# The beginning of a hybrid block kernel, rebuilt: statistics tile by tile, normalisation and splitting on two engines, small loads moved

## The reference, cut to what matters

```
h = layer_norm(concat(pad, meta, x), ln_in_g, ln_in_b)
proj = h @ w_in[l]                       # XM, OG, i, f, QA, KA, VA, GA, GB
y_m = mlstm_branch(xm, o_pre, i_pre, f_pre, ...)
y_a = diff_attn_branch(qa, ka, va, ...)
merged = sigmoid(ga) * (y_m @ w_branch_m) + sigmoid(gb) * (y_a @ w_branch_a)
h = layer_norm(DN_ALPHA * h + merged @ w_out, ln1_g, ln1_b)
ffn = group_moe(h, w_router, router_bias, w_gate_e, w_up_e, w_down_e)   # 16 experts
h = layer_norm(DN_ALPHA * h + ffn, ln2_g, ln2_b)
```

## Time and profile before

| what | value |
|---|---|
| median of 3 runs | 835.6 us (834.52 to 838.2) |
| the profiled execution, its time | 835.89 us |
| its span | 834.1 us |
| PE busy | 779.0 us, 93% |
| DVE, ACT, POOL busy | 357.6, 240.8, 22.7 us |
| read from HBM | 249.91 MB, 301 GB/s over the span |

### The profile page before, as it was taken

One profiled execution on the slowest core, in us unless ns is written; L12 is line 12 of the kernel. 1 busy time (PEld: TensorE's weight loads), 2 busy tenths in 40 slices (PEclk: granted clock), 3 DMA queues, 4 the chain that ended last, 5 costly groups with the idle time before them and its releaser, 6 DMA issues.

```text
span 834.1 us, 12681 instructions
## 1 busy us (share of the span) xinstructions
PE 779.0 (93%) x4496; PEld 474.1 (57%) x4497; DVE 357.6 (43%) x780; ACT 240.8 (29%) x523; POOL 22.7 (3%) x51
## 2 busy tenths in 40 slices
PE   4999999999999999998999999889999998898993
PEld 3998679999889999783333333333333333333331
DVE  6677436554665787636223212230223202312225
ACT  2454433444766655431111011101111111011010
POOL 2002000000001000000000000000000000000000
PEclk9999999999999999979999999999999999999997
DMA  8965050553105433995999999999999999999971
GB/s 252 388 233 200 2 202 2 201 199 139 68 1 202 152 130 151 393 384 240 429 427 428 427 427 428 428 428 429 429 428 427 428 429 429 428 427 427 427 329 50
DMA packets 36764, 251.30 MB, mean 301 GB/s; under 512 B 5921, under 2 KB 13170, under 8 KB 23426
## 3 DMA queue, kind: packets, MB, share of 16 engines
q1 hardware_dynamic: 34416, 250.76, 73.0%
q10 hardware_dynamic: 2322, 0.21, 0.2%
HBM read 249.91 MB, written 1.05 MB: 301 GB/s over the span
## 4 chain that ended last, share of the span: by engine, by line
PE 71%; DMA 21%; DVE 3%; ACT 2%; issue 2%; POOL 1%; DVEq 0%; POOLq 0%; SPq 0%; ACTq 0%
PE ps L1952 26%; DMA raw<-in_w_down_e_dram 21%; PE ps L1617 8%; PE ps L1619 7%; PE ps L1618 7%; PE ps L1905 2%; PE ps L1913 2%; PE ps L1673 1%; PE ps L1920 1%; PE ps L1669 1%; PE ps L1729 1%; PE ps L1592 1%; PE ps L1868 1%; PE ps L1870 1%; PE ps L1869 1%
## 5 line engine op out<-in xcount | busy, mean ns | idle before, releaser
L1952 PE MATMUL ps<-raw,hid 128*64 128x512 f32 x512 | 119.6, 618 | 19.4 <-DMA raw<-in_w_down_e_dram 18.9
L1617 PE MATMUL ps<-hi_h,whi 128*128 128x256 f32 (+1 forms) x448 | 129.8, 290 | 3.8 <-DVE wlo L983 3.7
L1619 PE MATMUL ps<-hi_h,wlo 128*128 128x256 f32 (+1 forms) x448 | 127.5, 285 | 0.0
L1618 PE MATMUL ps<-lo_h,whi 128*128 128x256 f32 (+1 forms) x448 | 127.2, 284 | 0.0
L1952 PE MATMUL ps<-raw,xg 128*64 128x512 f32 x512 | 112.7, 592 | 1.7 <-DVE xg L1413 1.7
L983 DVE TENSOR_TENSOR wlo<-raw,whi 128x512 fp32r<-128x512 f32 x144 | 93.4, 690 | 46.7 <-ACT whi L688 44.1
L1544 DVE TENSOR_TENSOR gs<-ps,gsig 128x512 f32<-128x512 f32 x16 | 11.1, 692 | 183.0 <-ACT gsig L930 182.2
L1617 PEld LDWEIGHTS ps<-hi_h,whi 128*128 128x128 f32 x448 | 84.4, 188 | 8.3 <-DVE wlo L983 4.8
L1952 PEld LDWEIGHTS ps<-raw,hid 128*64 128x64 f32 x512 | 36.7, 141 | 92.0 <-issue 65.3
L688 ACT CAST whi<-raw 128x512 fp32r<-128x512 f32 (+1 forms) x144 | 83.2, 618 | 13.2 <-PE ps L1619 11.9
L1619 PEld LDWEIGHTS ps<-hi_h,wlo 128*128 128x128 f32 x448 | 84.5, 189 | 0.0
(11 more groups left out here) (321 smaller groups left out, 1017.9 us busy)
## 6 DMA issues: line engine op xcount, KB each, us to landing
raw<-in_w_down_e_dram SPq DMA_DIRECT2D x32, 2048.0 KB, 21.2
raw<-in_w_gate_e_dram SPq DMA_DIRECT2D x16, 2048.0 KB, 25.7
raw<-in_w_up_e_dram SPq DMA_DIRECT2D x16, 2048.0 KB, 23.8
gate_x<-in_w_gate_e_dram SPq DMA_DIRECT2D x16, 2048.0 KB, 27.2
raw<-in_w_in_dram SPq DMA_DIRECT2D x28, 1024.0 KB, 9.2
up_x_right<-in_w_up_e_dram SPq DMA_DIRECT2D x16, 1024.0 KB, 27.6
up_x_left<-in_w_up_e_dram SPq DMA_DIRECT2D x8, 2048.0 KB, 25.2
raw<-in_w_branch_m_dram SPq DMA_DIRECT2D x4, 1024.0 KB, 8.1
```

The source lines that it names most:

```text
L1617: mm(o, w1, hi[:, k, c0:c0 + n], start=(k == 0), stop=False)
L1618: mm(o, w1, lo[:, k, c0:c0 + n], start=False, stop=False)
L1619: last = mm(o, w2, hi[:, k, c0:c0 + n], start=False, stop=(k == KB - 1))
L1952: last = mm(ps[r0:r0 + SLOTS, bank_no, :], lhs[:, k % 4, k // 4, :], w[:, k % 2, 512 * c:512 * c + 512], start=(k == 0), stop=(k == KB - 1))
```

## The change

On DVE the statistics of the meta tile and the first token tile go ahead, and POOL raises these two (in one instruction over 128 rows) while DVE takes the third tile's. The first token tile is normalised by ACT, with the bias `nmr0`, the other two by DVE. ACT's mask casts come first. The first weight block is split ahead of the tokens on both engines. `hfull` has four buffers; DVE makes the even ones and ACT the odd ones. On PE `keep_warm` stands ahead of the transposes, which write other banks, and the first block waits for `lo_h` one k at a time. The split of `wif`, the sums for `lams` and the waits for them stand behind XM's stream. The nine small loads go from ACT's queue to SP's, between XM's quarters and `rows_in`; the residual (`hres`) comes one block later. Its core as a diff:

```diff
     rows_in = at("rows_in", [P, 2, D], F + 12288)
-    hfull = at("hfull", [P, 2, S], F + 20480)
+    HB = 4
+    hfull = at("hfull", [P, HB, S], F + 55616)
+    nmr0 = at("nmr0", [P, 1], F + 59968)
...
-                sp.wait_ge(raw_in[0][0], 16)
+                with nc.allow_non_contiguous_dma(reason="a few short vectors"):
+                    sp.dma_start(wif[:], w_in[0, :, 2048:2056].rearrange("(k p) c -> p k c", p=P)).then_inc(s.wif_in, 16)
+                    sp.dma_start(gate_bias[:, 0:1], b_i.rearrange("a h -> h a")).then_inc(s.gb_in, 16)
+                    sp.dma_start(gate_bias[:, 1:2], b_f.rearrange("a h -> h a")).then_inc(s.gb_in, 16)
+                    for tile, v in ((gain4, ln1_g), (bias4, ln1_b)):
+                        sp.dma_start(tile[:], v[0].rearrange("(c i a) -> i c a", c=2, a=4)).then_inc(s.gain4_in, 16)
+                for j, v in enumerate((lam_q1, lam_q2, lam_k1, lam_k2)):
+                    sp.dma_start(lamv[:, j, :], v[0].partition_broadcast(P)).then_inc(s.lam_in, 16)
                 for j, v in enumerate((ln_in_g, ln_in_b)):
                     sp.dma_start(rows_in[:, j, :], v.partition_broadcast(P)).then_inc(s.rows_in_in, 16)
...
+        pool.wait_ge(s.var_ready, 2)
+        pool.tensor_tensor(rstd[:, 0:2], ve[:, 0:2], minus_half[:, 0:2], ALU.pow).then_inc(s.rstd_ready, 1)
         pool.wait_ge(s.var_ready, 3)
-        pool.tensor_tensor(rstd[0:META, 0:1], ve[0:META, 0:1], minus_half[0:META, 0:1],
-                           ALU.pow).then_inc(s.rstd_ready, 1)
-        pool.tensor_tensor(rstd[:, 1:3], ve[:, 1:3], minus_half[:, 1:3], ALU.pow).then_inc(s.rstd_ready, 1)
+        pool.tensor_tensor(rstd[:, 2:3], ve[:, 2:3], minus_half[:, 2:3], ALU.pow).then_inc(s.rstd_ready, 1)
 
...
-        with nc.allow_non_contiguous_dma(reason="a few short vectors"):
-            for tile, v in ((gain4, ln1_g), (bias4, ln1_b)):
-                act.dma_start(tile[:], v[0].rearrange("(c i a) -> i c a", c=2, a=4)).then_inc(s.gain4_in, 16)
-            act.dma_start(wif[:], w_in[0, :, 2048:2056].rearrange("(k p) c -> p k c", p=P)).then_inc(s.wif_in, 16)
-            act.dma_start(gate_bias[:, 0:1], b_i.rearrange("a h -> h a")).then_inc(s.gb_in, 16)
-            act.dma_start(gate_bias[:, 1:2], b_f.rearrange("a h -> h a")).then_inc(s.gb_in, 16)
-        for j, v in enumerate((lam_q1, lam_q2, lam_k1, lam_k2)):
-            act.dma_start(lamv[:, j, :], v[0].partition_broadcast(P)).then_inc(s.lam_in, 16)
-
-        for k in range(KB):
-            act.wait_ge(s.h_full, k + 1)
-            act.copy(hi_h[:, k, :], hfull[:, k % 2, :]).then_inc(s.h_hi, 1)
+        act.wait_ge(s.consts, 1)
+        for narrow, wide in ((ident_b, ident), (late_b, late), (ahead_b, ahead), (before_b, before)):
+            act.copy(narrow[:], wide[:]).then_inc(s.masks_ready, 1)
+        act.wait_ge(s.nmr0_ready, 1)
+        act.activation(xt[:, 1, :], xt[:, 1, :], ACT.Identity, bias=nmr0[:], scale=rstd[:, 1:2]).then_inc(s.x1_ready, 1)
+
...
+        def full_half(k):
+
+            act.wait_ge(s.ht_t, k + 1)
+            if k >= HB:
+                act.wait_ge(s.h_lo, k - HB + 1)
+            act.activation(hfull[:, k % HB, :], ps[:, 4 + k % 4, 0:S], ACT.Identity, bias=chan[:, C_LNB + k:C_LNB + k + 1],
+                           scale=chan[:, C_LNG + k:C_LNG + k + 1]).then_inc(s.h_odd, 1)
+
+        def high_half(k):
+            act.wait_ge(s.h_odd if k % 2 else s.h_even, k // 2 + 1)
+            act.copy(hi_h[:, k, :], hfull[:, k % HB, :]).then_inc(s.h_hi, 1)
+
+        act.wait_ge(s.chan_ready, 1)
+        for k in range(0, KB, 2):
+            full_half(k + 1)
+            high_half(k)
+            high_half(k + 1)
+
+        stream(XM, OG)
+
         act.wait_ge(s.wif_in, 16)
-        act.wait_ge(s.consts, 1)
-        for narrow, wide in ((ident_b, ident), (late_b, late), (ahead_b, ahead),
-                             (before_b, before)):
-            act.copy(narrow[:], wide[:]).then_inc(s.masks_ready, 1)
         act.copy(wif_hi[:, :, 0:MH], wif[:, :, MH:2 * MH]).then_inc(s.wif_split, 1)
         act.copy(wif_hi[:, :, 32:32 + MH], wif[:, :, 0:MH]).then_inc(s.wif_split, 1)
-
-
-        stream(XM, OG)
-
         act.wait_ge(s.lam_sum, 1)
         act.activation(lams[:, 2:4], lams[:, 0:2], ACT.Exp).then_inc(s.lam_exp, 1)
...
+        rows = (META, P, P)
+
+        def tile_stats(j):
+            n = rows[j]
             dve.wait_ge((s.x_in0, s.x_in1, s.x_in2)[j], 16)
             for c in range(2):
                 own(dve.bn_stats(stats[0:n, j, c, :], xt[0:n, j, 512 * c:512 * c + 512]))
...
+
+        def tile_mean(j):
+            own(dve.bn_aggr(mv[0:rows[j], j, :], stats[0:rows[j], j, :, :]))
+
+        def tile_var(j):
+            dve.tensor_scalar(ve[0:rows[j], j:j + 1], mv[0:rows[j], j, 1:2], EPS, None, ALU.add).then_inc(s.var_ready, 1)
+
+        def tile_norm(j):
+            n = rows[j]
             dve.tensor_scalar(xt[0:n, j, :], xt[0:n, j, :], mv[0:n, j, 0:1], rstd[0:n, j:j + 1],
                               ALU.subtract, ALU.mult).then_inc(s.xn_ready, 1)
+
+        tile_stats(0)
+        tile_stats(1)
+        own.settle()
+        tile_mean(0)
+        tile_mean(1)
+        own.settle()
+        dve.wait_ge(s.consts, 1)
+        tile_var(0)
+        tile_var(1)
+        tile_stats(2)
+        dve.wait_ge(s.rstd_ready, 1)
+        dve.scalar_tensor_tensor(out=nmr0[:], in0=mv[:, 1, 0:1], scalar=-1.0, in1=rstd[:, 1:2], op0=ALU.mult,
+                                 op1=ALU.mult).then_inc(s.nmr0_ready, 1)
+        own.settle()
+        tile_mean(2)
+        own.settle()
+        tile_var(2)
+        tile_norm(0)
         dve.wait_ge(s.rows_t, 1)
-        dve.tensor_copy(chan[:], ps[:, 7, 0:81]).then_inc(s.chan_ready, 1)
+        dve.tensor_copy(chan[:], ps[:, 3, 0:81]).then_inc(s.chan_ready, 1)
+        dve.wait_ge(s.rstd_ready, 2)
+        tile_norm(2)
         dve.wait_ge(s.chan_ready, 1)
         own(dve.tensor_scalar(chan[:, C_AG:C_AG + 1], chan[:, C_AG:C_AG + 1], 1.0 - LAM_INIT, None, ALU.mult))
 
 
+        def full_half(k):
+
+            dve.wait_ge(s.ht_t, k + 1)
+            dve.tensor_scalar(hfull[:, k % HB, :], ps[:, 4 + k % 4, 0:S], chan[:, C_LNG + k:C_LNG + k + 1],
+                              chan[:, C_LNB + k:C_LNB + k + 1], ALU.mult, ALU.add).then_inc(s.h_even, 1)
+
         def low_half(k):
             dve.wait_ge(s.h_hi, k + 1)
-            dve.tensor_tensor(lo_h[:, k, :], hfull[:, k % 2, :], hi_h[:, k, :].bitcast(F32),
+            dve.tensor_tensor(lo_h[:, k, :], hfull[:, k % HB, :], hi_h[:, k, :].bitcast(F32),
                               ALU.subtract).then_inc(s.h_lo, 1)
 
...
         def split(section, blk, odd):
 
             for kh in range(2):
...
         split(XM, 0, 0)
-        dve.wait_ge(s.wif_split, 2)
-        for a, b in ((0, MH), (32, 0)):
-            own(dve.tensor_tensor(wif_lo[:, :, a:a + MH], wif[:, :, b:b + MH],
-                                  wif_hi[:, :, a:a + MH].bitcast(F32), ALU.subtract))
-        own.settle()
-        dve.sem_inc(s.wif_split, 1)
-
-        dve.wait_ge(s.lam_in, 64)
-        own(dve.tensor_tensor(lamp[:], lamv[:, 0:2, :], lamv[:, 2:4, :], ALU.mult))
-        own.settle()
-        dve.tensor_reduce(lams[:, 0:2], lamp[:], AX.X, ALU.add).then_inc(s.lam_sum, 1)
-
+        full_half(0)
+        full_half(2)
+        for k in range(0, KB, 2):
+            low_half(k)
+            low_half(k + 1)
+            if k + HB < KB:
+                dve.wait_ge(s.h_lo, k + 1)
+                full_half(k + HB)
...
+            n = blk - 3
...
-                dve.wait_ge(s.xn_ready, t + 2)
+                dve.wait_ge(s.xn_ready, 2)
+                dve.wait_ge(s.x1_ready, 1)
                 dve.tensor_tensor(hres[:, t, :], xt[:, t + 1, :], rows_in[:, 0, :], ALU.mult).then_inc(s.hres_scaled, 1)
 
         stream(XM, OG, residual)
 
+        dve.wait_ge(s.wif_split, 2)
+        for a, b in ((0, MH), (32, 0)):
+            own(dve.tensor_tensor(wif_lo[:, :, a:a + MH], wif[:, :, b:b + MH],
+                                  wif_hi[:, :, a:a + MH].bitcast(F32), ALU.subtract))
+        own.settle()
+        dve.sem_inc(s.wif_split, 1)
+
+        dve.wait_ge(s.lam_in, 64)
+        own(dve.tensor_tensor(lamp[:], lamv[:, 0:2, :], lamv[:, 2:4, :], ALU.mult))
+        own.settle()
+        dve.tensor_reduce(lams[:, 0:2], lamp[:], AX.X, ALU.add).then_inc(s.lam_sum, 1)
+
+        dve.wait_ge(s.masks_ready, 4)
...
-        pe.wait_ge(s.xn_ready, 3)
+        pe.transpose(ps[:, 3, 0:81], crow[:], ident[0:81, 0:81]).then_inc(s.rows_t, 1)
+        keep_warm(2, 16)
+        pe.wait_ge(s.xn_ready, 2)
+        pe.wait_ge(s.x1_ready, 1)
         for k in range(KB):
             if k >= 4:
-                pe.wait_ge(s.h_full, k - 3)
+                pe.wait_ge(s.h_odd if k % 2 else s.h_even, (k - 4) // 2 + 1)
             c = slice(P * k, P * k + P)
-            pe.transpose(ps[:, k % 4, 0:META], xt[0:META, 0, c], ident[0:META, 0:META])
```

(24 more changed lines are left out.)

54 lines of the change are left out of this document (21 added, 33 removed).

## The result

The changed kernel takes 830.88 us (median of 6 runs, 829.26 to 832.18), the kernel before 835.12 us on the same chip (6 runs, 832.76 to 838.2). The medians are 4.2 us apart, 0.5%. The ratio of the runs is 0.9942, with an interval of 0.9918 to 0.9967, so the change is faster, by some 0.6%. The profiled execution took 831.87 us with a span of 830.1, which is 4.0 less than before. The time forecast was 832.4, in a range of 829.6 to 835.2.

What follows compares the result with a forecast made beforehand. PE, busy for 93% of the span, was taken as the bound. From the profiled 835.9 us, -6.3 (XM earlier) +1.4 (OG) +1.7 (clock) = -3.2 gave 832.7, or 832.4 against the median, in a range of 829.6 to 835.2.

Steps and rivals of the forecast that it cites:

- T: Start of the first transpose on PE, forecast at 13.2 us, right behind `keep_warm`, 1.2 us later than before.
- The statistics: DVE, POOL and ACT ahead of the transposes: tiles ready at 10.8, 1.2 us earlier, worth nothing because `keep_warm` hides them.
- The give-back at OG: Between XM and OG: `wif` and `lams` work, formerly free, now costs 1.4 us, bounds nothing and 1.5.
- ACT's wait for `lam_sum`: Sign to look for behind XM's last evacuation: ACT waits about 1.1 us for `lam_sum`.
- absolute date behind OG: Stages behind OG: none found whose start doesn't depend on PE, so the shift should reach the end.
- T + 7.5: End of XM's first block, 0.4 us behind the last `lo_h`; 20.9 instead of 27.2, so XM ends 6.3 us earlier.
- 0.2 more for the second block's weights: XM's second block: its weights are split only behind the first block's `lo_h`, put at 0.2 us.
- I expect it to fall behind them, and XM's first block to run partly at 1.2 GHz: 1.7 us: PE's clock falls behind the transposes, slowing XM's first block; cost 1.7 us, bounds nothing and 3.4.
- the fall at 361: Earlier clock fall at about 361 us, behind transposes and short products during which PE counts as busy.
- the first rival: The clock holds from the transposes into XM, no 1.7 us loss: 831.0, or 830.7 at the median; chance 0.30.
- the third: Shift swallowed by a later stage's own start or dearer clock falls; time stays 834 to 836.5, chance 0.13.
- The small loads: SP's queue ahead of OG's quarters: counted as nothing, 3.4 us of room before OG's fourth quarter is needed at 40.2.

Runs made afterwards that it cites:

- old_stats: Changed kernel with statistics and normalisation as before the change, all three tiles normalised by DVE; one run, 830.83 us.
- aside: Changed kernel with the `wif` and `lams` work put among XM's blocks instead of behind XM; 828.67 us, ratio 0.9926 to the kernel before.
- transposes3: Changed kernel with each group of transposes issued three times into the same bank; one run, 836.37 us.
- no_warm: Changed kernel without the 16 products of `ident` (`keep_warm`) ahead of the transposes; 832.09 us, ratio 0.9959 to the kernel before.
- warm8: Changed kernel with 8 instead of 16 products of `ident` in `keep_warm`; 830.0 us, ratio 0.9937 to the kernel before.
- dve_full: Changed kernel with all eight `hfull` made by DVE again, ACT only casting, four buffers kept; one run, 830.43 us.
- after_again: The changed kernel itself with no edit, measured again on another chip; 831.38 us, ratio 0.9951 to the kernel before.
- small_on_act: Changed kernel with the nine small loads back on ACT's queue, at the beginning; one run, 831.09 us.
- warm_behind: Changed kernel with `keep_warm` back behind the transposes, all else as changed; 835.89 us, ratio 0.9986 to the kernel before.
- aside_warm10_fill: `aside_warm10` plus 3 and 5 products of `ident` in PE's two waits at the router; 828.65 us, ratio 0.9911 to the kernel before.
- aside_warm10: `aside` with 10 instead of 16 products of `ident` in `keep_warm`; 829.61 us, ratio 0.9928 to the kernel before.
- whole_lo: Changed kernel, but PE waits for all eight `lo_h` before XM's first product; one run, 838.23 us.

## Why the forecast came out as it did

**Held.** `keep_warm` holds the transposes: T 13.24, forecast 13.2. The statistics are hidden under it: the tiles were ready at 9.98 (forecast 10.8), and `old_stats` shows that they are worth nothing there. The give-back at OG is 1.46 (forecast 1.4, bounds 0 and 1.5), and `aside` shows that it is paid in full. ACT's wait for `lam_sum` is 1.12 (forecast 1.1). There is no absolute date behind OG that swallows the shift: 5.41 us at OG's end are 5.5 at the turning of `h1`.

**Mis-sized.** The step "T + 7.5" for the first block, with 0.2 more for the second block's weights. XM ended 6.86 us earlier, not 6.3. The forecast let the splitting set the first block's end, with the last `lo_h` at T + 7.1. It was done at T + 6.25 (19.49), since two `lo_h` take 0.78 us together and not 1.01, and a pair of k 1.17 and not 1.5. What sets the end is PE: eight groups of transposes at 0.53 take 4.1 us, 24 products at 0.126 take 3.0, together 7.1, and the evacuation follows at T + 7.36. PE is the bound itself, because the clock was up for the transposes. Laid out from the two timelines, XM's first product comes 6.89 us earlier by 5.65 of `keep_warm` no longer behind the transposes, and 2.47 by the transposes at full clock, less 1.23 for the later T. The 2.47 is a term that the forecast did not have; it had the first block's 3.0 hidden under the splitting in its place. When DVE makes all `hfull`, the splitting does set it, at T + 8.19.

**Failed.** The step "I expect it to fall behind them, and XM's first block to run partly at 1.2 GHz: 1.7 us". The clock held through the transposes and all of XM. The row it was drawn from was read too widely: 6.5 us of transposes had not raised a low clock, and I took this to say that they let a high one fall. `transposes3` separates the two. The other row, the fall at 361, was behind transposes too, but behind short products between waits as well; it doesn't say which of them counted. One of its readings was off as well, without effect: the products of `ident` were at the low clock until 23.0 (4.4 us behind 18.54), not until about 22.

**Why the total was near all the same.** A clock loss of the same 1.7 us came at another place, the first expert's products (8.79 against 7.09). From the profiles: -6.86 at XM, +1.46 at OG, +1.7 at 374, which makes -3.7; measured -4.0, the rest in small steps between. The forecast had -6.3, +1.4, +1.7. So the number is near in part by luck: the first rival (the clock holds, 831.0) described the beginning, and the third (falls at dearer places) described the router, at its smallest price. Against the medians the forecast was further off: 830.88 was measured, the forecast said 832.4, and the first rival 830.7, with a chance of 0.30. The time below 831.4 had a chance of 0.38.

That loss goes with the low stretches; that it belongs to the change as such is not shown, and `aside`, with the same beginning, has the length of the kernel before. From the turning of `h1` to the second expert's gather it takes 31.29 us before (386.18 less 354.89) and 32.91 after. Over the profiles of all kernels this length falls into steps, and it follows the time that the granted clock is low between 350 and 385 us:

| length, us | clock low, us | kernels |
|---|---|---|
| 29.7 | 6.8 | `no_warm`, `transposes3` |
| 31.2 to 31.3 | 10.2 | before, `warm8`, `aside`, `dve_full` |
| 32.7 to 33.0 | 13.7 | changed, `after_again`, `old_stats`, `small_on_act`, `warm_behind`, `aside_warm10_fill` |
| 34.6 | 17.1 | `aside_warm10`, `whole_lo` |

None of these edits, apart from `aside_warm10_fill`'s, touches that part of the program. From the first length to the last it is 4.95 us in three steps, 1.65 each for 3.4 us more at the low clock, the price of one short low stretch. So the low clock accounts for the lengths; what sets its time is open. They mask gains of that size: `warm8` ends OG 1.8 us earlier than the changed kernel and has a median 0.9 lower (on another chip).

**The small loads.** Right in the result, close in the room. OG's quarters are issued 2.6 us later (20.26 against 17.66). `wif` and the first `gate_bias` hold SP for 2.83 and 3.46 us, until 16.1, but that is not what the move cost: in the kernel before SP was held as well, until 16.8, by the plain `rows_in`, the first load behind XM's quarters there:

```profile
11.77 5.02 SPq L460 DMA_DIRECT2D rows_in<-in_ln_in_g_dram  x1
```

Nearly all of the delay is the issue time of the other seven, 3.2 us (16.12 to 19.31), less the 0.7 by which SP was free earlier. In the changed kernel's DMA view the fourth is

```profile
raw<-in_w_in_dram SPq DMA_DIRECT2D x1, 1024.0 KB, 14.9
```

issued at 23.9: it lands at 38.8, not at 36.8, and is needed at about 39.6. Of the 3.4 us of room 0.8 are left. In `warm8` they are used up: ACT's cast of OG's first block stands idle for 1.21 us, until 39.08, as the quarter lands. OG's end is 1.83 us earlier all the same (66.89), as is XM's, so even there it set nothing.

**What stays open.** Why the low stretches at the router come where they do was not shown: the filled waits and the vanished second stretch are one profile each with and without, and later stretches changed along with it. The beginnings, too, are single profiles of each kernel, and no run has the old statistics behind a shorter `keep_warm`. Nor was `whole_lo`'s wait filled, which would tell whether the clock falls there without idleness.

## What to carry to other kernels

Look at what stands in the bounding engine's own queue before pricing anything on others: here a filler of 6.4 us hid all gains in statistics and normalisation, and in one profile half of it did the same job. Look for edits that need each other: with the filler back behind the transposes XM ends 4.4 us later, and with PE waiting for all operands at once, in place of one k at a time, it takes 5 us longer from T. Either one taken away leaves 2.3 to 2.5 of the 6.9 us at XM's end, so the two can't be added. Work that was free behind a filler isn't free in its new place: put it among the blocks of a stream, not at its end, where it cost 1.5 us in full.

## What was unexpected in the hardware

- **Transposes held a clock that they had not raised.** 12.5 us of them at full pace with the clock up (`transposes3`), 6.4 to 6.5 us of them without a rise with the clock down (before, `no_warm`). Behind them the clock fell 1.2 us into a wait of 2.25 and stayed down for 6.8 us (`whole_lo`); the fall at 558.9 came 0.5 us behind the end of a wait of 2.1. Whether the transposes had a part in the fall of `whole_lo` is open. In `warm8` the clock rose 1.5 us into the transposes, with 3.7 us of `ident` products ahead of them.
- **The date of the rise varies.** `keep_warm` starts at 6.91 to 7.04 in the changed kernel, `after_again` and `old_stats`, and the clock rises at 12.3, 11.3 and 10.3. T moves with it: 13.24, 12.80, 12.36. The Trainium skill ("TensorE: Matmul & The Clock Gate", Part 1: The HAM clock gate) says that the number of matmuls at the low clock differs between runs of one kernel; these three agree. It is why experiments on this beginning are compared from T on.
- **The first loads behind large ones hold the queue, whatever their size.** Behind XM's four quarters of 1 MB SP was held by `wif` and the 4 numbers of `gate_bias` for 2.83 and 3.46 us, and in their absence by `rows_in` for 5.02 (before) and 5.61 (`small_on_act`); each time it was free at 16.1 to 16.8. On ACT's queue, with nothing large ahead of them there, the same `wif` and `gate_bias` took 0.49 and 0.50 (before). That the quarters' unfinished work does it fits these dates, and no run isolates it.
